# Weight sums and a gate product moved from GpSimd to VectorE, fourteen weight pairs back to eight block products, and a new order of stages

## The reference

```python
h = rmsnorm(x, norm_g)
a_val, a_gate, z_a, gb, gc, hb, z_b = split(h @ w_in)      # 7 x 1024 columns
u  = a_val * sigmoid(a_gate)
ca = head_layernorm(causal_dwconv(u, width 31) + bias)     # 8 heads of 128 channels
y_a = silu(ca) * silu(z_a)
v  = gc * hb
y_b = gb * causal_dwconv(v, width 3) * silu(z_b)
x  = x + concat(y_a, y_b) @ w_out                          # w_out: 2048 x 1024
```

## Time and profile before

| | |
|---|---|
| time, median of 3 runs | 1175.58 us (1174.46 to 1176.99) |
| profiled execution | 1176.52 us |
| its span, slowest core (core 7) | 1175.0 us (cores 1160.3 to 1175.0) |
| busy: TensorE, VectorE, ScalarE, GpSimd | 1055.2, 787.1, 700.1, 623.3 us |
| mean granted TensorE clock, core 7 | 0.970 |

### The profile page before, as it was taken

The page is one execution under the profiler, slowest core; times in us unless marked ns, Lnnn a source line. Parts: engine busy times, 40 slices in busy tenths (PEclk is TensorE's granted clock), DMA queues, the critical chain, the costliest instruction groups (busy, mean ns, idle before and its releaser), DMA issues.

```text
span 1175.0 us, 21181 instructions; the slowest of 8 cores (1160.3 to 1175.0 us)
## 1 busy us (share of the span) xinstructions
PE 1055.2 (90%) x6706; PEld 513.4 (44%) x6706; DVE 787.1 (67%) x1296; ACT 700.1 (60%) x1149; POOL 623.3 (53%) x718
## 2 busy tenths in 40 slices
PE   5888889999898997999999899999889999939997
PEld 2343444445444443445444444444444444424455
DVE  3587697798876995444335789788789879712333
ACT  5856677687777774322152577797578767512332
POOL 6567566655656774322252777565566647502342
PEclk8989999999999999899999999999999999969999
DMA  9647757756666649934332765865746584950445
GB/s 225 163 95 102 117 79 133 125 97 110 130 98 116 103 81 166 202 136 157 136 88 56 125 112 88 163 113 90 141 68 108 95 146 70 208 112 27 144 144 179
DMA packets 185805, 142.45 MB, mean 121 GB/s; under 512 B 140000, under 2 KB 152160, under 8 KB 185632
## 3 DMA queue, kind: packets, MB, share of 16 engines
q0 software_dynamic: 34352, 54.97, 30.5%
q1 hardware_dynamic: 150912, 85.58, 29.9%
q10 hardware_dynamic: 432, 0.55, 0.1%
HBM read 149.08 MB, written 43.79 MB: 164 GB/s over the span
## 4 chain that ended last, share of the span: by engine, by line
PE 57%; DVE 11%; issue 10%; ACT 9%; DMA 7%; POOL 5%; DVEq 0%; ACTq 0%; POOLq 0%; SPq 0%
PE psb L717 29%; PE psb L940 25%; DMA wsl<-w_in_r 3%; DVE tmp L1227 3%; ACT toep L1019 2%; DMA wsl<-w_out_r 2%; POOL tmp L1243 2%; DMA big<-w_out_r 1%; POOL wsum L921 1%; DVE big L1065 1%; ACT tmp L1224 1%; PE psb L1045 1%; PE psb L1382 1%; DVE u_sb L870 1%; PE psb L1046 1%
## 5 line engine op out<-in xcount | busy, mean ns | idle before, releaser
L717 PE MATMUL psb<-h_sb,wsl 128*128 128x64 bf16 (+1 forms) x1664 | 220.1, 282 | 14.7 <-ACT tmp L1145 6.2
L940 PE MATMUL psb<-h_sb,wsum 128*128 128x512 bf16 x672 | 165.6, 386 | 21.5 <-DVE psb L961 19.7
L940 PE MATMUL psb<-xst,wsum 128*128 128x512 bf16 x672 | 170.7, 385 | 15.5 <-POOL wsum L921 6.2
L940 PE MATMUL psb<-h_sb,wsl 128*128 128x512 bf16 x672 | 174.8, 385 | 7.5 <-ACT tmp L860 3.7
L1019 ACT ACTIVATE toep<-wt_sb 32x512 bf16<-32x512 bf16 x256 | 160.0, 625 | 25.8 <-PE psb L1046 9.8
L717 PEld LDWEIGHTS psb<-h_sb,wsl 128*128 128x128 bf16 x1664 | 110.3, 99 | 124.8 <-issue 29.6
L1227 DVE SCALAR_TENSOR_TENSOR tmp<-vbuf,cw_b_sb,tmp 128x512 f32<-128x512 bf16 (+1 forms) x160 | 135.8, 849 | 34.1 <-POOL vbuf L1187 16.3
L1303 DVE TENSOR_TENSOR xst<-xst,psb 128x512 f32<-128x512 f32 (+2 forms) x80 | 44.8, 566 | 151.0 <-PE psb L717 129.6
L1243 POOL TENSOR_TENSOR tmp<-tmp 128x512 f32<-128x512 f32 (+1 forms) x80 | 93.1, 1164 | 98.5 <-DVE tmp L1227 78.6
L755 ACT ACTIVATE tmp<-xst 128x1024 bf16<-128x1024 f32 (+2 forms) x44 | 38.8, 881 | 164.7 <-DVE xst L1303 158.0
L921 POOL TENSOR_TENSOR wsum<-wsl 128x512 bf16<-128x512 bf16 x84 | 110.2, 1324 | 44.1 <-PE psb L940 17.9
(11 more groups left out here) (154 smaller groups left out, 1949.0 us busy)
## 6 DMA issues: line engine op xcount, KB each, us to landing
wsl<-w_in_r POOLq DMA_DIRECT2D x112, 256.0 KB, 6.2
scr_u<-u_sb SPq DMA_DIRECT2D x16, 704.0 KB, 5.8
up_sb<-scr_u SPq DMA_DIRECT2D x16, 704.0 KB, 6.5
scr_c<-big SPq DMA_DIRECT2D x16, 640.0 KB, 6.6
big<-scr_c SPq DMA_DIRECT2D x16, 640.0 KB, 6.3
wt_sb<-wt_d POOLq DMA_DIRECT2D x64, 128.0 KB, 3.6
xst<-x_d SPq DMA_DIRECT2D x16, 512.0 KB, 6.0
x_mid<-xst SPq DMA_DIRECT2D x16, 512.0 KB, 2.7
```

Of the source, the lines that this page charges most:

```text
L717: ins = e.matmul(bank(v, n), lhsT=l_(), rhs=r_(), start=(first and i == 0), stop=(last and i == len(pairs) - 1))
L940: ins = e.matmul(bank(v, 512), lhsT=lhs(k), rhs=rhs(k), start=first and k == 0, stop=True if not first else k == 3, skip_group_check=not f ...
```

## The change

- Weight sums (`sums`) go to VectorE (`SDVE` holds all four).
- `GPOOL` is false: in `pb_b` VectorE multiplies B by silu(z_B), and then by the taps. GpSimd has no part in it.
- `WK` names the pairs of each layer that keep the seven-product form. The others (a1, b0 to b5, b7 in layer 0; b0 to b5 in layer 1) go through the new `plain`: eight products, in which blocks 1 and 3 still use a sum of the weight's halves together with the differences of h that `t_forms` leaves in place.
- `TACT` 3 and not 4: one of the four Toeplitz copies of each build is VectorE's.
- The planner's assumed durations, priorities (`BG`), step orders, stage order, `OUTQ` and `ZQ` are new.

```diff
 ORDER = [
-    "C0 b0 C1 a1 Z0 P2 b1 Z1 C2 P3 a2 P4 C3 b2 Z2 P5 a3 C4 b3 Z3 Z4 P6 C5 a4 C6 P7 C7 b4 a5 b5 Z5 a6 b6 a7 Z6u0 b7u1 Z7up",
-    "C0 b0 C1 a1 Z0 P2 b1 P3 C2 P4 a2 Z1 b2 C3 P5 Z2 C4 a3 P6 b3 Z3 Z4 C5 a4 b4 a5 C6 Z5 P7 C7 b5 a6 b6 a7 Z6u0 Z7u1 b7up",
+    "C0 b0 a1 b1 C1 Z0 P2 C2 Z1 P3 a2 C3 P4 b2 P5 Z2 C4 a3 b3 P6 Z3 Z4 C5 C6 a4 P7 b4 C7 Z5 a5 b5 a6 b6 a7 Z6u0 b7u1 Z7up",
+    "C0 b0 a1 b1 C1 P2 C2 Z0 Z1 P3 Z2 a2 P4 C3 b2 P5 C4 a3 b3 P6 Z3 Z4 C5 a4 P7 C6 C7 b4 Z5 a5 b5 a6 b6 Z6u0 a7 b7u1 Z7up",
 ]
-STEPSP = "P10 P50 P60 P11 P20 P51 P61 P30 P21 P70 P40 P31 P71 P41 s"
+STEPSP = "P10 P50 P60 P30 P51 P11 P20 P61 P21 s P31 P70 P40 P71 P41"
...
-YPOOL, GPOOL, TACT, LSQ = False, True, 4, 1
+YPOOL, GPOOL, TACT, LSQ = False, False, 3, 1
-OUTQ = (0, 1, 4, 2, 3)
+OUTQ = (2, 0, 1, 3, 4)
-ZQ = (3, 0, 1, 2, 4)
-BG = {"p": -300, "halo": 30, "sd": -300, "yb": -100, ...}
+ZQ = (0, 4, 2, 3, 1)
+SDVE = (0, 1, 2, 3)
+C22B = False
+WK = ['P0 P1 P2 P3 P4 P5 P6 P7 a0 a2 a3 a4 a5 a6 a7 b6', 'P0 P1 P2 P3 P4 P5 P6 P7 a0 a1 a2 a3 a4 a5 a6 a7 b6 b7']
+BG = {"sd": -300, "p5b": 30, "co": 30, "y": 300, "hist": -300, "sz": -100, ...}
...
     def c_act(n, ptr=0, sbuf=False):
-        return 0.1 + (0.1 if sbuf else 0.0) + 0.045 * ptr + n * 0.000833
+        return (0.2 if sbuf else 0.168) + 0.092 * ptr + n * 0.000833
     def c_dve(n, rate=1, ptr=0):
-        return (0.07 if rate == 1 else 0.16) + 0.05 * ptr + n / 960.0 / rate
+        return 0.155 + 0.05 * ptr + n / 960.0 / rate
...
         def add(i, a, b, rd):
-            S.op("pool", (lambda e: e.tensor_tensor(out=ap(i), in0=a(), in1=b(), op=ALU.add)), 0.95, rd, [parts[i]], lock=True, holds=[s], name=f"S{i}")
+            fn = (lambda e: e.tensor_tensor(out=ap(i), in0=a(), in1=b(), op=ALU.add))
+            if i in SDVE:
+                dve(fn, 512, rd, [parts[i]], rate=2, lock=True, holds=[s], name=f"S{i}")
+            else:
+                S.op("pool", fn, 1.15, rd, [parts[i]], lock=True, holds=[s], name=f"S{i}")
...
+    def plain(w1, w2, f1, f2, nm, **kw):
+        s = V("sum")
+        parts = rs(2)
+        for i, w in ((0, w1), (1, w2)):
+            fn = (lambda e, i=i, w=w: e.tensor_tensor(out=wsum[:, s.slot, 512 * i:512 * i + 512], in0=wh(w, 0), in1=wh(w, 1), op=ALU.add))
+            if i in SDVE:
+                dve(fn, 512, [w], [parts[i]], rate=2, lock=True, holds=[s], name=f"S{i}")
...
+        def one(i, w, q):
+            if q not in (1, 3):
+                return proj(w, q, name=f"{nm}{i}.{q}", **kw)
+            v = V("bank", "proj", "full")
+            pairs = [((lambda k=k: w_ap(w, k)), (lambda k=k: hv(k, q))) for k in range(4)] + \
+                [((lambda k=k: wsum[:, s.slot, 512 * i + 128 * k:512 * i + 128 * k + 128]), (lambda k=k: hv(4 + k, q))) for k in range(4)]
+            held = kw.get("holds", []) + [s]
+            mm("proj", v, 512, pairs, [w, parts[i]] + [h_r[k][q] for k in range(KC)], **{**kw, "holds": held}, name=f"{nm}{i}.{q}")
+            return v
+        for q in range(NB):
+            f1(q, one(0, w1, q))
+            f2(q, one(1, w2, q))
...
-            pair(wz, wb, f1, f2, f"b{j}", **y.kw())
...
+        (pair if f"b{j}" in WK[l] else plain)(wz, wb, f1, f2, f"b{j}", **y.kw())
```

More of the change, by code:

```diff
@@ L870, in p1_val @@
             dve((lambda e, blk=blk: e.scalar_tensor_tensor(out=blk(u_blk(ub, q)), in0=blk(b4(tm(th, n), q)), scalar=1.0, in1=blk(b4(sv(bv, n), q)),
-                                                           op0=ALU.add, op1=ALU.mult)), n if i is None else n // 2, [bv, th], [u_r[ub][q]], name=f"u{j}.{q}")
+                                                           op0=ALU.add, op1=ALU.mult)), n if i is None else n // 2, [bv, th], [u_r[ub][q]], lock=bv.pool == "snap", name=f"u{j}.{q}")
         def fn(e):
@@ L926, in sums @@
         return s, parts
+    def plain(w1, w2, f1, f2, nm, **kw):
[5 more added lines that the diff above has]
+                dve(fn, 512, [w], [parts[i]], rate=2, lock=True, holds=[s], name=f"S{i}")
+            else:
+                S.op("pool", fn, 1.15, [w], [parts[i]], lock=True, holds=[s], name=f"S{i}")
+        def one(i, w, q):
[10 more added lines that the diff above has]
+            f2(q, one(1, w2, q))
     def pair(w1, w2, f1, f2, nm, **kw):
@@ L970, in step @@
                 prod(d["a"], sk(2), hk(q2, 0), [sr[2]] + hr4(q2, 0), False, [s], f"P7{nm}.{i}")
-                dve((lambda e: e.tensor_tensor(out=tm(d["c"], 512), in0=bank(d["a"], 512), in1=tm(d["c"], 512), op=ALU.subtract)),
-                    512, [d["a"], d["c"]], [d["c"]], name=f"c22{nm}.{i}")
-                f2(q2, d["c"])
+                to = d["b"] if C22B else d["c"]
+                dve((lambda e: e.tensor_tensor(out=sv(to, 512), in0=bank(d["a"], 512), in1=tm(d["c"], 512), op=ALU.subtract)),
+                    512, [d["a"], d["c"]], [to], name=f"c22{nm}.{i}")
+                f2(q2, to)
             else:
@@ L1129, in ln_z @@
         col = l * 8 + j
-        if WINO:
+        if PAIRS:
             zs = V("zsum")
-            S.op("pool", (lambda e: e.tensor_tensor(out=zsum[:, zs.slot, 0:512], in0=wh(w, 0), in1=wh(w, 1), op=ALU.add)), 0.95, [w], [zs],
+            S.op("pool", (lambda e: e.tensor_tensor(out=zsum[:, zs.slot, 0:512], in0=wh(w, 0), in1=wh(w, 1), op=ALU.add)), 1.15, [w], [zs],
                  lock=True, name=f"Sz{j}", **y.kw())
@@ L1139, in ln_z @@
                 n, [cn, vecs_r], [s], ptr=2, sbuf=True, name=f"s{j}.{q}", **y.kw())
-            if WINO and q in (1, 3):
+            if PAIRS and q in (1, 3):
                 bz = proj_t(w, zs, q, after=[cn_of[(l, j, "op")]], name=f"z{j}.{q}", **y.kw())
@@ L1166, in pb_h @@
         dve((lambda e: e.tensor_tensor(out=v_blk(q, 0), in0=b3(sv(bh, n), q), in1=b3(tm(th, n), q), op=ALU.mult)),
-            n, [bh, th], [v_r[q]], name=f"vb{j}.{q}")
+            n, [bh, th], [v_r[q]], lock=bh.pool == "snap", name=f"vb{j}.{q}")
         if q == 3:
@@ L1191, in p1, with f1 @@
         wg, wv = w_load(w_in_r[l, 8 + j]), w_load(w_in_r[l, j])
[L1192 to L1200, removed]
+        ths = {}
+        def f1(q, v):
+            ths[q] = p1_gate(j, q, v)
+        (pair if f"P{j}" in WK[l] else plain)(wg, wv, f1, lambda q, v: p1_val(j, q, v, ths[q]), f"P{j}")
         p1_end(l, j)
@@ L1204, in pb_a, with f1 @@
         wc, wx = w_load(w_in_r[l, 32 + j]), w_load(w_in_r[l, 40 + j])
[L1205 to L1213, removed]
+        ths = {}
+        def f1(q, v):
+            ths[q] = pb_c(l, j, q, v)
+        (pair if f"a{j}" in WK[l] else plain)(wc, wx, f1, lambda q, v: pb_h(l, j, q, v, ths[q]), f"a{j}")
         pb_a_end(l, j)
@@ L1249, in f2g @@
             dve((lambda e: e.tensor_tensor(out=y.ap(q), in0=sv(v, n), in1=tm(sz, n), op=ALU.mult)),
-                n, [v, sz], [y.res[q]], after=y.after, name=f"yb{j}.{q}", **y.kw())
+                n, [v, sz], [y.res[q]], after=y.after, lock=v.pool == "snap", name=f"yb{j}.{q}", **y.kw())
         def f2(q, v):
@@ L1254, in f2 @@
             sz = szs[q]
-            dve((lambda e: e.tensor_tensor(out=tm(sz, n), in0=sv(v, n), in1=tm(sz, n), op=ALU.mult)), n, [v, sz], [sz], name=f"gz{j}.{q}")
+            dve((lambda e: e.tensor_tensor(out=tm(sz, n), in0=sv(v, n), in1=tm(sz, n), op=ALU.mult)), n, [v, sz], [sz], lock=v.pool == "snap", name=f"gz{j}.{q}")
             a = taps(q)
```

15 lines of the change are left out of this document (5 added, 10 removed).

## The result

The changed kernel takes 1117.57 us (median; 1115.81 to 1119.67). Its ratio to the kernel before is 0.9508, 95% interval 0.9487 to 0.9528, 58 us faster. The forecast was 1154.6 us with a range from 1128 to 1182: right in direction, and too small by a factor of 2.8.

What follows compares the result with a forecast made beforehand. TensorE was nearest to the bound, with VectorE making it wait. Chain savings of 49 us, counted as 33, against 24.2 us of added matmuls gave -9; ends and start -12; -21 in all: 1154.6 us, range 1128 to 1182.

Steps and rivals of the forecast that it cites:

- the copies on VectorE would hold back weight loads: A rule read for the 64 moved Toeplitz copies: each could delay a weight load by a fraction of a microsecond.
- VectorE, made shorter: VectorE's operations with two SBUF operands, slowed beside GpSimd: 90 us of excess, of which 75 us should go.
- the small groups: VectorE's short tree steps, mean and rstd products, u and v from SBUF: 35 us of contention excess.
- VectorE stays about as full: VectorE's busy time, 787 us before, would come to 806 us: added work traded one for one against relief.
- pricing the hold-up and the hops by their share of the chain: Savings over the chain's entries: product 11, sums 8, contention 12, Toeplitz copies 6, plain pairs 12; together 49 us.
- The discount of a third: Next waits come up behind those taken away, so only two thirds of the chain savings count: 33 us.
- TensorE's added 24 us: Fourteen plain pairs add 112 matmuls of 512 columns at 0.216 us on TensorE: 24.2 us, charged in full.
- The new order: Stage reordering: layer 1's end hides about 7 us of w_out wait, layer 0's end 0; with the start, -12 us.
- Rival C: Slower: VectorE is the bound in disguise, saved waits don't come back; 1190 us, range 1179 to 1200, chance 0.19.
- rival B: More gain: full 49 us counts and half of two long DMA waits goes; 1131 us, range 1115 to 1140, chance 0.24.
- B's two reasons: First, waits don't come up behind, so all 49 us count; second, half of the long DMA waits' 40.8 us goes.
- the 49 us: Sum of the savings over the chain's entries, before two thirds of it, 33 us, were counted.

Runs made afterwards that it cites:

- b_sg: Kernel before with weight sums and gate product on VectorE; no plain pairs, Toeplitz copies on ScalarE, old durations and orders: ratio 0.9627, 1132 us.
- a_dummy: Changed kernel with useless SBUF-reading additions on GpSimd behind its instructions in the mixed stages, instruction order kept: ratio 0.9956, 1170 us.
- a_dummy_set: Changed kernel with useless memsets on GpSimd that read nothing, two in place of each useless addition, order kept: ratio 0.9691, 1139 us.
- b_s: Kernel before with the weight sums alone on VectorE; gate product on GpSimd, all 42 pairs in seven products, old durations and orders: ratio 0.9927, 1167 us.
- b_plain: Kernel before with the fourteen plain pairs alone; sums, gate product, Toeplitz copies, durations and orders as before: ratio 1.0010.
- a_old_both: Changed kernel with the old assumed durations and the old orders and priorities, so only the work is new: ratio 0.9559, 1124 us.
- b_sg_plain: Kernel before with sums and gate product on VectorE plus the fourteen plain pairs; Toeplitz copies on ScalarE, old durations and orders: ratio 0.9755, 1147 us.
- b_costs: Kernel before with only the planner's new assumed durations; same work and stage order: ratio 1.0278, 1208 us.
- b_order: Kernel before with only the new stage order, step orders, priorities, OUTQ and ZQ; old durations and work: ratio 1.0549, 1240 us.

## Why the prediction was wrong

**Right.** The direction, and the counts: 112 more matmuls, GpSimd at 314.7 us (forecast 306), ScalarE at 633.6 (627). Single durations too: sums 0.43 (0.425), Toeplitz copies 0.306 (I took 0.4), the tap sum 0.748 (0.75), y_a's product somewhat longer than forecast, 0.732 (0.69). The two subtractions removed were 57.9 + 57.1 - 38.6 - 38.4 = 38.0 us (38.6). That the copies on VectorE would hold back weight loads does not show: the 112 issues of such loads take 0.545 us each (0.555 before), and the loads land 5.6 us after them (6.2 before).

**Mis-sized: VectorE, made shorter.** I took 75 us out of an excess of 90. By the measured durations (the product at the forecast's 47 us) VectorE would be at 787.1 + 59.1 (sums) + 47 + 19.6 - 38.0 = 875 us; it is at 762. So 113 us of hold-up went. I had L1227 right (26 us), but put the small groups at 35 together: the short tree steps, the products with mean and rstd, and v, u and the state rows from SBUF had been slowed by more than that. And I left a sixth of the excess to the rest of GpSimd's work. "VectorE stays about as full" did not hold: its busy time fell by 25 us while it took on 126 us of work and gave up 38.

**The step that failed: pricing the hold-up and the hops by their share of the chain.** From the earlier trace rows I gave contention 12 us, the product 11, the sums 8, the plain pairs 12, the copies 6, and then took two thirds of the sum, 33 us. The runs show in its place: moving sums and product alone, under the old plan's settings, brings 44 us where this step had 31 before the discount (b_sg; with the Toeplitz copy, the plain pairs or both added, 40, 29 and 52). In one fixed order, useless work on GpSimd costs 53 us (a_dummy), 31 of them by the hold-up itself (a_dummy against a_dummy_set). That is 31 us for 89 us of VectorE's time, where I had 12 for 75. TensorE's idle time in the mixed stretches fell by 57 us, where I had 33.

The traces suggest why the share was too low. A chain of waits that goes through four engines in microsecond pieces gives each engine only the pieces that came last, and the delay that a slow instruction leaves to those queued behind it appears under other names. In the fixed order the hold-up raised "issue" and ScalarE's share as well as VectorE's. In the changed kernel "issue" is at 2% and not 10, and ScalarE at 2% and not 9, though its instructions take as long as before (a Toeplitz copy 0.626 us, then 0.625) and it has only a tenth less of work.

The discount of a third, for waits that come up behind, has no support in the runs either. b_s brings 9 us and b_sg 44, so the product, moved second, brought 35, though it takes less time off GpSimd (93 against 224 us). Undone in the changed kernel it is the other way round: the product costs 20 us, the sums on top of it 80. What one of the two is worth depends on the other and on the plan.

**TensorE's added 24 us** were subtracted in full. Plain pairs alone cost nothing and bring nothing (b_plain 1.001). So there what they relieve, with the higher clock and the new plan, pays for the matmuls in full, where I had 12 us of relief for 24 us of matmuls. A gain of their own is not shown: on top of b_sg the time was 15 us more, or 8 less with the Toeplitz copy and the locks.

**The new order.** I gave it 12 us, for the ends and the start. The wait on w_out at the end of layer 1 went from 24.35 to 19.23 us, 5 where I had 7; the chain in the changed kernel:

```profile
426.88 21.62 DMA wsl<-w_in_r
...
967.28 19.23 DMA wsl<-w_out_r
```

At the end of layer 0 a wait of 21.62 us on a load of w_in stands where there was one of 16.47 on w_out; as I had taken, nothing is won there. Orders and durations together brought 6 us (a_old_both to the changed kernel). Rival C did not come about. The result lies in rival B's own range (1115 to 1140), in part by luck. Of B's two reasons the second fell, since the two long DMA waits stayed (40.8 us before, 40.9 after). The first, that the waits do not come up again behind each other, would have given only the 49 us less 24; more came because the 49 themselves were priced too low.

**Open.** How much of the last 14 us (1132 to 1118) belongs to plain pairs, Toeplitz copies, durations and orders: their effects lie below what another plan alone makes, up to 23 us between b_sg_plain and a_old_both and 33 to 65 us in b_costs and b_order. The 44 us of b_sg hold such an effect too. The gate product alone under the old plan was not run, so how the 44 us split between sums and product is shown only in one sequence. The mean granted clock rose from 0.971 to 0.984 on both dies (medians of their cores), and how much of the gain comes by it is not known.

## What to carry to other kernels

Where two engines hold each other up, don't price the relief by their share of the chain of waits: add the hold-up over all groups (the mean of each form against its undisturbed duration) and expect a good part of it at the end. Here it was 31 us for 89 us of VectorE's time, in one kernel and one order. Useless work with the order kept measures such a cost without disturbing the order, and two kinds of it separate the hold-up from the mere occupation. Undoing the parts of a tuned kernel can overstate them, here three times over, probably since the plan was fitted to the whole; add each alone to the kernel before as well.

## What was not expected

Assumed durations nearer the measured ones (b_costs: ScalarE's 512 columns from PSUM 0.594 assumed against 0.593 measured, formerly 0.527) made the old kernel 2.8% slower. The planner with truer numbers need not give a better plan; it may be that the old orders were fitted to the old numbers, which no run shows. And memsets on GpSimd, which read nothing, still lengthened VectorE's Toeplitz copies from 0.306 to 0.342 us while L1260 stayed at 0.749.
